# Expert choice of tokens on one core: the top-k by two lists of five and three tiles in place of four and four

## The reference, cut to what matters

```python
def ec_moe(h, router, w1, w3, w2):
    bn, N, _ = h.shape
    cap = CAP_FACTOR * N // N_EXPERTS          # 128 of 1024 latent tokens, 16 of 128 context tokens
    aff = jax.nn.softmax(jnp.einsum('bnd,de->ben', h, router).astype(F32), axis=1)
    gate, idx = lax.top_k(aff, cap)
    bidx = jnp.arange(bn)[:, None, None]
    xs = h[bidx, idx]
    hid = jax.nn.silu(jnp.einsum('becd,edf->becf', xs, w1)) * jnp.einsum('becd,edf->becf', xs, w3)
    out = jnp.einsum('becf,efd->becd', hid, w2) * gate[..., None].astype(h.dtype)
    return jnp.zeros_like(h).at[bidx, idx].add(out)
```

## Time and profile before

| | us |
|---|---|
| median of 3 runs | 4610.81 |
| lowest, highest | 4610.56, 4611.62 |
| the profiled execution's own time | 4608.15 |
| its span | 4606.3 |
| PE busy | 4273.0 (93%) |
| DVE busy | 1268.7 (28%) |
| ACT busy | 673.1 (15%) |
| POOL busy | 215.7 (5%) |

### The profile page before, as it was taken

How to read it: one execution, slowest core, us unless ns; L and a number is a source line. 1 busy time by engine, 2 the same in 40 slices (tenths; PEclk the granted TensorE clock), 3 DMA queues, 4 the chain that set the end, 5 groups by cost and what they waited for, 6 DMA issues and landing times. The chain is left out here.

```text
span 4606.3 us, 61875 instructions
## 1 busy us (share of the span) xinstructions
PE 4273.0 (93%) x27077; PEld 3718.8 (81%) x27077; DVE 1268.7 (28%) x3038; ACT 673.1 (15%) x1677; POOL 215.7 (5%) x122
## 2 busy tenths in 40 slices
PE   8899988989968999999996799999987999999995
PEld 4667775577438999999996688888647999999995
DVE  5324452254380000000003432533472000000003
ACT  0022221100221110110111211111231101110111
POOL 0000000000220000000001000000120000000001
PEclk8999999999989999999998899999988999999998
DMA  7221001031326788878776311010324777777776
GB/s 283 109 77 29 22 3 29 28 136 58 110 92 237 287 308 290 305 284 312 285 288 213 101 32 33 15 45 14 138 105 165 276 282 278 280 269 282 277 274 209
DMA packets 148567, 790.12 MB, mean 172 GB/s; under 512 B 14792, under 2 KB 51304, under 8 KB 102410
## 3 DMA queue, kind: packets, MB, share of 16 engines
q1 hardware_dynamic: 139082, 752.60, 44.1%
q0 software_dynamic: 9216, 33.56, 3.5%
HBM read 729.92 MB, written 56.20 MB: 171 GB/s over the span
## 5 line engine op out<-in xcount | busy, mean ns | idle before, releaser
L1731 PE MATMUL PS<-arena 128*128 128x144 f32 x11264 | 1442.0, 287 | 6.5 <-ACT arena L1766 6.5
L1731 PEld LDWEIGHTS PS<-arena 128*128 128x128 f32 x11264 | 1407.3, 191 | 7.5 <-ACT arena L1766 7.3
L1716 PE MATMUL PS<-arena 128*128 128x144 f32 x5632 | 743.4, 286 | 0.0
L1716 PEld LDWEIGHTS PS<-arena 128*128 128x128 f32 x5632 | 711.5, 190 | 4.5 <-issue 4.5
L1824 DVE TENSOR_TENSOR arena<-PS,arena 128x144 f32<-128x144 f32 x352 | 108.2, 308 | 2004.0 <-ACT arena L1792 2004.0
L1792 ACT ACTIVATE arena<-PS 128x144 f32<-128x144 f32 x352 | 102.2, 290 | 1716.0 <-PE PS L1731 1716.0
L2053 PE MATMUL PS<-arena 128*128 128x256 f32 x1152 | 262.4, 388 | 21.6 <-DVEq L2306 11.0
L2053 PEld LDWEIGHTS PS<-arena 128*128 128x128 f32 x1152 | 221.9, 195 | 52.8 <-issue 22.9
L1367 PE MATMUL PS<-arena 128*128 128x512 f32 x576 | 259.2, 605 | 5.5 <-PEq L2350 5.0
L1367 PEld LDWEIGHTS PS<-arena 128*128 128x128 f32 x576 | 109.2, 194 | 131.8 <-issue 130.7
L600 ACT ACTIVATE arena<-PS,arena 128x128 f32<-128x128 f32 (+1 forms) x480 | 176.2, 470 | 236.4 <-PE PS L1684 124.7
(11 more groups left out here) (308 smaller groups left out, 3576.5 us busy)
## 6 DMA issues: line engine op xcount, KB each, us to landing
arena<-expert_panels SPq DMA_DIRECT2D x352, 1536.0 KB, 6.6
arena<-ada_w SPq DMA_DIRECT2D x6, 4096.0 KB, 14.4
arena<-ada_w SPq DMA_DIRECT2D x12, 2048.0 KB, 12.2
arena<-odd_w_in SPq DMA_DIRECT2D x16, 1024.0 KB, 5.5
arena<-hgrn_w SPq DMA_DIRECT2D x20, 512.0 KB, 4.1
arena<-filter_spectra SPq DMA_DIRECT2D x36, 256.0 KB, 2.7
mid_rows<-arena SPq DMA_DIRECT2D x18, 512.0 KB, 2.9
arena<-h_rows SPq DMA_DIRECT2D x18, 512.0 KB, 4.7
```

What stands on the lines that cost most here:

```text
L1716: m = pe.matmul(PS[:, m_ // 3, m_ % 3 * SLOTS:m_ % 3 * SLOTS + SLOTS], s.w2[n % RING][:, m_ * P:(m_ + 1) * P], s.hid[:, f, :], start=f == ...
L1731: m = pe.matmul(PS[:, 6 + n % 2, q * 256:q * 256 + SLOTS], s.w13[n % RING][:, q, k, :], s.xs[e % 2][:, k, :], start=k == 0, stop=k == KD - 1)
```

## The change

The lower list takes tiles 0 to 4 and is 640 wide, the upper one tiles 5 to 7 and is 384 wide. Since tile 4's affinities come in step 6, the lower list's rounds start in step 6: five in step 6, five in step 7, three in step 8, and the last three behind the last tile, ahead of the upper list's. Both lists keep their 16 rounds, and the number of instructions is the same on every engine.

```diff
-        HALF = L_LAT // 2
+        HALF = 5 * P
...
-                    if i >= 5:
-                        s.rounds(dve, ch, first, s.val[0], s.ind[0], done, min(done + 3, 16))
-                        done = min(done + 3, 16)
+                    if i >= 6:
+                        s.rounds(dve, ch, first, s.val[0], s.ind[0], done, done + 3)
+                        done += 3
                     ch.link(s.dve_half(dve, ch, i, 1))
                     s.dve_norm(dve, ch, i)
                     if i:
                         s.dve_softmax(dve, ch, i - 1)
-                    if 5 <= i < NT - 1:
+                    if 6 <= i < NT - 1:
                         s.rounds(dve, ch, first, s.val[0], s.ind[0], done, done + 2)
                         done += 2
-                assert done == 16
                 s.dve_aff(dve, ch, NT - 2)
                 dve.wait_ge(s.tf, NT)
                 for k in range(4, KD):
                     m = modulate_tile(dve, s.uT[(NT - 1) % 2][:, k, :], PS[:, 5, k % 4 * P:k % 4 * P + P], s.l, 2, k, False, False)
                 m.then_inc(s.ud, 1)
+                s.rounds(dve, ch, first, s.val[0], s.ind[0], done, 16)
                 ch.link(dve.tensor_copy(s.pos[0], s.ind[0]))
                 s.rounds(dve, ch, last, s.val[1], s.ind[1], 0, 3)
```

## The result

| | before | changed |
|---|---|---|
| median of 10 runs each, us | 4610.53 | 4622.28 |
| lowest, highest | 4607.23, 4612.50 | 4619.97, 4631.14 |
| the profiled execution's own time | 4608.15 | 4619.97 |
| its span | 4606.3 | 4618.2 |

The ratio is 1.003, with a 95% interval of 1.002 to 1.0039: slower by 11.75 us in the medians, where 15.2 were forecast. The forecast time, 4626.0, is 3.7 us above the measured one. The range of 4622 to 4630 holds the measured median by only 0.28 us. The means of the ten runs, 4623.86 and 4610.19, lie 13.7 us apart.

A forecast was written before the change was run, and what follows sets the result against it. DVE was taken to bound the token-choice stage from step 5 on. Per layer -3.18 + 17.18 - 6.42 = +7.58 us, two layers +15.2, on 4610.81 gives 4626.0 us; range 4622 to 4630.

The forecast's parts named there:

- Where the stage turns from PE to DVE: Token choice, loop over tiles: DVE bounds from step 5 on, where rounds filled its wait for PE's projection.
- Round prices: Straight line through widths 128 and 512: 2.554 us a round at 640, 1.752 at 384, together 4.31.
- Step 6 early by 3.18: Without rounds in step 5, step 6 starts when its projection is there, at 1287.47 in place of 1290.65.
- lower list +17.18: From step 6 on, 16 rounds of 640 (40.86 us) replace 11 of 512 (23.68 us): 17.18 us more a layer.
- upper list -6.42: Behind the last tile, 16 rounds at 1.752 in place of 2.153 us: 6.42 us less a layer, all on the path.
- The waits that could open: Context-row trips keep 1.2 us of cover; last half's projection ends over 6 us ahead of its reader: cost nothing.
- TensorE's clock: Against a clock falling a step earlier: PE's waits in step 7 stay and the one in step 6 goes.
- third rival: Step 8's projections and transposes at 1.2 GHz: last projection takes 14.1 us, ends 4.6 us late, kernel 4635.2; chance 0.03.

The follow-up runs named there:

- Schedule alone: Changed kernel with lists of four and four tiles, lower list's rounds still starting in step 6: 4624.59 us against 4609.25 before, ratio 1.0034.
- Widths alone: Kernel before with lists of five and three tiles, rounds still starting in step 5, affinities zeroed first: 4608.93 us against 4609.25, ratio 1.0.
- second comparison: The unaltered change run again beside the kernel before on the same chip: 4622.85 us against 4609.67, ratio 1.003.
- a further attempt: Kernel with rounds inside the softmax, plus one round moved ahead of the first half's scaled sum in steps 6 to 8: 4599.36 us against 4600.01 without.

## Why the prediction was right, and what was off

*Where the stage turns from PE to DVE.* Right. Step 5 has its 5.38 us wait back and step 6 starts 16.50 us behind step 5 (16.51 forecast).

*Round prices.* 2.554 forecast and 2.55 measured for 640; 1.752 and 1.75 for 384. The straight line holds on both sides of 512. The Trainium skill (VectorE: DVE Perf Modes, Side-by-side: where the cycles go) had led to an estimate of 0.831 and 0.565 us for one instruction; the trace shows 0.81 to 0.82 and 0.55 for the maximum, so its straight line is confirmed and its level is 2 to 3% high here.

*Step 6 early by 3.18, lower list +17.18, upper list -6.42.* Their sum, +7.58, was measured as +7.47 and +7.50. The second half of step 8 came 70.05 us behind the start of step 5, before 63.73: 6.32 later, 6.34 forecast. The missing 0.1 us is a term that I left out: the cast L1561 takes 0.21 us now, and took 0.31 before, when POOL's last residual operation was still running.

*Decomposition.* Schedule alone: all of the loss but 0.1 us a layer. Widths alone: none. Removing step 5's rounds: 3.3 of 10.8 us. Each part was tested by itself, so this is shown.

*The waits that could open.* None did in the change. DVE takes the context columns at 3479.05 in layer 1, at once behind its rounds. PE had ended them 1.98 us earlier, where 1.2 us of cover were forecast; the matmuls L1434 ahead of them took 5.81 us in place of 6.57. In layer 0 the cover was 1.28. The experts' first transposes moved with the last cast, to 0.4 us in layer 0 and 0.1 in layer 1.

*TensorE's clock.* Here a sentence of mine was wrong, if harmless. I wrote that PE's waits in DVE's step 7 stay. PE runs ahead where DVE begins early in step 6, so its wait ahead of step 8's first transposes grew from 1.44 to 3.08 us, and in layer 0 the clock was lower behind it. The third rival came true in part, and without its price: the first projection of step 8 still took 7.11 us, and the second 7.42, not the 14.1 of the rival. The 7.4 us between the projection's end and its reader absorbed that.

*The step that was off* is the last one, from the stage to the kernel: two layers at 7.58 were to give 15.2 us, and the medians gave 11.75, then 13.2 in the second comparison and 15.3 for the schedule alone. The two stages give 14.97 in the trace. The 95% interval of the first ratio, 1.002 to 1.0039, holds 1.0033. The profiles put the difference into stretches with unchanged work, which vary by some 4 us between executions of the same code. The means say it more plainly. They lie 13.7 us apart in the first comparison, 14.3 in the second, 15.5 for the schedule alone, where the two stages give 14.8. Each of these distances has a standard error of about 1 us, so no shortfall is established.

I had drawn the range from the medians' spread of 1.1 us over three runs. Over ten it is 5.3 before and 11.2 in the change, and in the later comparisons 9.5 over 22 runs before, 6.1 over eight of the change. A range from 4618 would have been the honest one. That the median lies 0.28 us inside the stated range, and not outside, was luck; that the mechanism was right was not. What sets an execution's time apart from the next by some 10 us stays open.

## What to carry to other kernels

Filler work has the price of its place: count the microseconds that it spends where its engine would be idle. A move that takes it out of an idle slot costs just that, where the work itself costs the same in sum, as the two lists did here. Find the step from which an engine no longer waits. Every microsecond of its work behind that step is on the path, and the order there is free as long as no wait opens. The idle slots inside it (here 1.60 us for an exponential, four times a stage) are worth filling until the other engine becomes the bound: of 6.4 us in those slots 5.0 were won, and a further attempt won 0.36. Balance such a split by the sum of loop and tail: a longer tail was free here when the loop gave back as much.

## What was not expected of the hardware

POOL can hold DVE up without a wait showing in the trace. A DVE operation with two inputs from SBUF, begun while POOL's two-input operation ran, was drawn as 1.64 and 2.13 us long in place of 0.69, and ended 0.54 to 0.56 us behind POOL's end. DVE's rounds, with one input each, ran at their normal time beside the same POOL operations, and so did L1478, with one of its inputs in PSUM: 0.69 us at 1306.43. Moving the operation behind POOL's end brought it back to 0.69. POOL's own time changed from 2.35 to 2.37 us. The Trainium skill (SBUF — State Buffer, 🔬 SBUF: two separate sides) says that DVE and GpSimd share a pair of ports that whoever comes first keeps for a whole instruction, and that a DVE operation with two SBUF inputs is one that needs it against a GpSimd operation that reads SBUF; the trace agrees, with these durations. That POOL is held up by DVE in the same way, no run here shows.

Small operations look like it. The last scaling of the softmax (L1506, 128x16) takes 0.49 us in the steps in which POOL's residual follows the norm, and 0.23 in the last softmax, when POOL is idle. In the kernel with the rounds inside the softmax the same operation took 0.31 us in step 5 and 0.23 in steps 6 to 8. In both kernels, wherever it took 0.31 us or more it ended 0.02 to 0.04 us behind the POOL operation that ran when it began; in steps 6 to 8 it began just as POOL's first operation ended. That this is the same cause was not tested by itself.
